# Up units of nine pairs per gated layer by Strassen's algorithm, all on VectorE, the x combinations made within the second pair

## The reference

```python
def _conv_glu_ffn(x, w_in, conv_w, conv_b, w_down):
    gate, up = jnp.split(x @ w_in, 2, axis=-1)
    gate = lax.conv_general_dilated(
        gate, conv_w[:, None, :], window_strides=(1,),
        padding=[(CONV_WIDTH // 2, CONV_WIDTH // 2)],
        ..., feature_group_count=FFN_DIM) + conv_b
    return (jax.nn.gelu(gate, approximate=False) * up) @ w_down

for i in range(DEPTH):
    ...
    h = _conv_glu_ffn(x, f_w_in[i], f_conv_w[i], f_conv_b[i], f_w_down[i])
    x = _layer_norm(DEEPNORM_ALPHA * x + h, ln_g[i, 1], ln_b[i, 1])
```

## Time and profile before

| | |
|---|---|
| median of 3 runs | 1276.72 us (1276.08 to 1278.55) |
| the profiled execution | 1277.31 us, its span 1275.6 us |
| TensorE busy | 1266.0 us (99%), 6096 matmuls |
| VectorE busy | 650.2 us (51%) |
| ScalarE busy | 459.4 us (36%) |
| GpSimd busy | 165.1 us (13%) |
| DMA, mean | 110 GB/s |

### The profile page before, as it was taken

The page is one execution under the profiler, slowest core; times in us unless marked ns, Lnnn a source line. Parts: engine busy times, 40 slices in busy tenths (PEclk is TensorE's granted clock), DMA queues, the critical chain, the costliest instruction groups (busy, mean ns, idle before and its releaser), DMA issues.

```text
span 1275.6 us, 15660 instructions
## 1 busy us (share of the span) xinstructions
PE 1266.0 (99%) x6096; PEld 1055.6 (83%) x6096; DVE 650.2 (51%) x890; ACT 459.4 (36%) x553; POOL 165.1 (13%) x159
## 2 busy tenths in 40 slices
PE   9999999999999999999999999999999999999997
PEld 7888888889888888888888877788988888888886
DVE  3637877346343434433372777775743334343346
ACT  3422333322232323322314588775143222232230
POOL 3001100040000000000224444453100000000001
PEclk9999999999999999999999999999999999999999
DMA  8434564250433232222522334235032333232221
GB/s 269 146 96 124 173 176 147 89 185 2 131 99 99 87 99 80 98 97 99 188 74 71 100 105 124 91 108 166 33 99 99 99 99 99 99 99 100 96 102 66
DMA packets 104652, 140.64 MB, mean 110 GB/s; under 512 B 9440, under 2 KB 81464, under 8 KB 104352
## 3 DMA queue, kind: packets, MB, share of 16 engines
q1 hardware_dynamic: 95024, 127.81, 31.2%
q0 software_dynamic: 9440, 12.11, 2.9%
q10 hardware_dynamic: 144, 0.13, 0.0%
HBM read 137.85 MB, written 10.52 MB: 116 GB/s over the span
## 4 chain that ended last, share of the span: by engine, by line
PE 98%; DVE 1%; DMA 0%; ACT 0%; issue 0%; POOL 0%; DVEq 0%; SPq 0%; POOLq 0%
PE bank L1263 31%; PE bank L1267 31%; PE bank L1266 31%; PE bank L1654 1%; PE bank L1508 1%; PE bank L1273 1%; PE bank L1406 1%; DMA w_raw<-in_a_w_in_dram 0%; PE bank L1511 0%; PE bank L1397 0%; DVE prob L1141 0%; DVE w_lo L875 0%; PE bank L1684 0%; PE bank L1683 0%; ACT w_hi L514 0%
## 5 line engine op out<-in xcount | busy, mean ns | idle before, releaser
L1263 PE MATMUL bank<-xt_hi,w_hi 128*128 128x512 f32 (+1 forms) x1008 | 380.8, 378 | 0.0
L1267 PE MATMUL bank<-xt_hi,w_lo 128*128 128x512 f32 (+1 forms) x1008 | 378.8, 376 | 0.0
L1266 PE MATMUL bank<-xt_lo,w_hi 128*128 128x512 f32 (+1 forms) x1008 | 378.7, 376 | 0.0
L765 DVE TENSOR_TENSOR w_lo<-w_raw,w_hi 128x2048 fp32r<-128x2048 f32 x79 | 180.8, 2289 | 184.6 <-ACT w_hi L468 158.3
L1263 PEld LDWEIGHTS bank<-xt_hi,w_hi 128*128 128x128 f32 x1008 | 189.7, 188 | 36.4 <-issue 3.0
L1267 PEld LDWEIGHTS bank<-xt_hi,w_lo 128*128 128x128 f32 x1008 | 189.7, 188 | 34.5
L1266 PEld LDWEIGHTS bank<-xt_lo,w_hi 128*128 128x128 f32 x1008 | 189.8, 188 | 33.9
L468 ACT CAST w_hi<-w_raw 128x2048 fp32r<-128x2048 f32 x53 | 101.3, 1913 | 185.6 <-PE bank L1263 179.6
L1263 PE MATMUL bank<-w_hi,s_hi 128*128 128x512 f32 x416 | 162.1, 390 | 0.0
L1266 PE MATMUL bank<-w_lo,s_hi 128*128 128x512 f32 x416 | 161.9, 389 | 0.0
L1267 PE MATMUL bank<-w_hi,s_lo 128*128 128x512 f32 x416 | 161.8, 389 | 0.0
(11 more groups left out here) (209 smaller groups left out, 1488.3 us busy)
## 6 DMA issues: line engine op xcount, KB each, us to landing
w_raw<-in_f_w_in_dram SPq DMA_DIRECT2D x44, 1024.0 KB, 5.1
w_raw<-in_f_w_down_dram SPq DMA_DIRECT2D x22, 1024.0 KB, 4.8
w_raw<-in_a_w_in_dram SPq DMA_DIRECT2D x14, 1024.0 KB, 6.1
bias_by_query_key<-bias_by_distance POOLq DMA_DIRECT2D x8, 1024.0 KB, 16.0
w_raw<-in_a_w_out_dram SPq DMA_DIRECT2D x8, 1024.0 KB, 7.0
w_raw<-in_b_w_qkv_dram SPq DMA_DIRECT2D x16, 512.0 KB, 4.8
bias_sb<-bias_by_query_key SPq DMA_DIRECT2D x32, 256.0 KB, 2.6
w_raw<-in_b_w_qkv_dram SPq DMA_DIRECT2D x4, 1024.0 KB, 5.4
```

Of the source, the lines that this page charges most:

```text
L765: dve.tensor_tensor(lo_of(u), w_raw[:, u % 2, :], hi_of(u), ALU.subtract).then_inc(w_lo_done, 1)
L1263: ins = pe.matmul(o, a_hi, b_hi, start=start, stop=False)
L1266: pe.matmul(o, a_hi, b_lo, start=False, stop=False)
L1267: return pe.matmul(o, a_lo, b_hi, start=False, stop=stop)
```

## The change

The first two pairs of each gated layer stay as they are (`PLAIN = 2`). In the other nine the up unit is one product of 2 x 2 cells: the weights [256 columns x 1024 rows] as cells A of 128 columns by 512 rows, x as cells of 512 rows by 256 tokens, the result as four quarters of 128 columns by 256 tokens. By Strassen's algorithm (Winograd's form) it takes seven cell products instead of eight, each 4 row chunks x 3 matmuls of 256 columns (`multiply`, banks 2 to 7 and again 2).

- Per pair VectorE makes four sums of weight cells (`sums`) and seven low parts (`lows`); ScalarE makes seven high parts and copies the first product (M1). VectorE adds the other products up out of PSUM into `act` (`add`, seven additions, the last one in the next pair), and multiplies `act` by the GELU in place (`gated`) in the next pair, between the sums and the low parts.
- Once per layer VectorE makes four combinations of x cells, T1 to T4, 1024 elements per partition each, in 10 operations that each wait for the one before; ScalarE makes their high parts and VectorE their low parts. In VectorE's queue the combinations stand in the second pair, behind the low part of its up unit and before its taps, the low parts behind the right taps and before the low part of the third gate unit. In ScalarE's queue the four high parts stand before the middle taps of the second pair.
- The loops are over seven pairs instead of ten, with the first and last of the nine written out. The down projection's start also waits for the sixth addition of the last pair.

Loads, the gate units and all other stages are unchanged. The diff, cut to its core:

```diff
+    w_sum = at("w_sum", 80 * KB, [P, 2, UC])
+    more_hi = [at(f"more_hi{k}", R_U + (72 + 2 * k) * KB, [P, NB], F32R) for k in range(3)]
+    more_lo = [at(f"more_lo{k}", R_U + (78 + 2 * k) * KB, [P, NB], F32R) for k in range(3)]
+    more_sum = [at(f"more_sum{k}", R_U + (78 + 2 * k) * KB, [P, NB]) for k in range(3)]
+    COMB = [R_U + 48 * KB, R_U + 56 * KB, 112 * KB, R_U + 64 * KB]
+    comb_hi = [at(f"comb_hi{k}", COMB[k], [P, KD // 2, 2 * P], F32R) for k in range(4)]
+    comb_lo = [at(f"comb_lo{k}", COMB[k] + 4 * KB, [P, KD // 2, 2 * P], F32R) for k in range(4)]
+    comb_part = [at(f"comb_part{k}", COMB[k], [P, KD // 2, 2 * P]) for k in range(4)]
+    comb = [at(f"comb{k}", COMB[k] + 4 * KB, [P, KD // 2, 2 * P]) for k in range(4)]
...
+        A11, A12, S1, S2, S4, S3, A22 = range(7)
+        T1, T2, T3, T4 = range(4)
+        M1, M2, M6, M7, M5, M3, M4 = range(7)
+        PLAIN = 2
+        NV = FB // 2 - PLAIN
+        def cell_sum(par, m):
+            return w_sum[:, par, NB * m:NB * m + NB] if m < 4 else more_sum[m - 4][:, :]
...
+        def raw_cell(par, b, a):
+            return w_raw[:, par, :].rearrange("p (k n) -> p k n", n=2 * P)[:, 4 * a:4 * a + 4, P * b:P * b + P]
+        def x_cell(xt, a, s):
+            return xt[:, 4 * a:4 * a + 4, 2 * P * s:2 * P * s + 2 * P]
+        def cell_bank(m):
+            return bank[(2, 3, 4, 5, 6, 7, 2)[m]][:, 0:2 * P]
...
+                def group(g):
+                    if g:
+                        weights_at(u0 + 2 * g + 1)
+                        for k in (T1, T2, T3, T4):
+                            act_e.wait_ge(comb_done, 4 * l + k + 1)
+                            act_e.copy(comb_hi[k][:, :, :], comb[k][:, :, :]).then_inc(comb_hi_done, 1)
...
+                    weights_at(u0 + 2 * g + 2)
+                    for j in range(2):
+                        gelu(2 * g + j, j)
...
+                    act_e.wait_ge(w_landed[par], landed_count(u) + (0 if i is None else i * 16))
+                    act_e.wait_ge(w_used, u - 1 + (0 if i is None else i * 2))
+                    for m, k in ((A11, 0), (A12, 1)):
+                        act_e.copy(as_cell(cell_hi(par, m)), raw_cell(par, 0, k)).then_inc(cell_hi_done, 1)
+                    for n, m in enumerate((S1, S2, S4, S3)):
+                        act_e.wait_ge(sum_done, count(l, 4, v, n + 1, i))
+                        act_e.copy(cell_hi(par, m), cell_sum(par, m)).then_inc(cell_hi_done, 1)
+                    act_e.copy(as_cell(cell_hi(par, A22)), raw_cell(par, 1, 1)).then_inc(w_hi_done, 1)
+                    for j in range(2):
+                        middle(f + j, j)
+                    act_e.wait_ge(cells_mm, count(l, 7, v, 1, i))
+                    act_e.copy(quarter(v, i, 1, 1), cell_bank(M1)).then_inc(m1_copied, 1)
+                    weights_at(u + 1, i)
+                    if v == NV - 1:
                         stationary(act, None, 0, act_done, f0 + 2)
+                    for j in range(2):
+                        gelu(f + j, j)
...
+                def step(ins, n):
+                    ins.then_inc(comb_step, 1)
+                    dve.wait_ge(comb_step, 6 * l + n)
+                def combine(k, hi, lo, n):
+                    whole, part = comb[k][:, :, :], comb_part[k][:, :, :]
+                    if k in (T1, T3):
+                        step(dve.tensor_tensor(whole, x_cell(xt_hi, *hi), x_cell(xt_hi, *lo), ALU.subtract), n)
+                        step(dve.tensor_tensor(part, x_cell(xt_lo, *hi), x_cell(xt_lo, *lo), ALU.subtract), n + 1)
+                        dve.tensor_tensor(whole, whole, part, ALU.add).then_inc(comb_done, 1)
+                    else:
+                        step(dve.tensor_tensor(whole, x_cell(xt_hi, *hi), comb[lo][:, :, :], ALU.subtract), n)
+                        dve.tensor_tensor(whole, whole, x_cell(xt_lo, *hi), ALU.add).then_inc(comb_done, 1)
+                    dve.wait_ge(comb_done, 4 * l + k + 1)
+                def group(g):
+                    if g:
+                        weights(u0 + 2 * g + 1)
+                    if g == 1:
+                        dve.wait_ge(up_mm, 2 * PLAIN * l + 2)
+                        combine(T1, (0, 1), (0, 0), 1)
+                        combine(T2, (1, 1), T1, 3)
+                    if g == 1:
+                        combine(T3, (1, 1), (0, 1), 4)
+                        combine(T4, (1, 0), T2, 6)
                     for j in range(2):
+                        left(2 * g + j, j)
                     for j in range(2):
+                        right(2 * g + j, j)
+                    if g == 1:
+                        for k in (T1, T2, T3, T4):
+                            dve.wait_ge(comb_hi_done, 4 * l + k + 1)
+                            dve.tensor_tensor(comb_lo[k][:, :, :], comb[k][:, :, :], comb_hi[k][:, :, :], ALU.subtract
+                                              ).then_inc(comb_lo_done, 1)
+                    weights(u0 + 2 * g + 2)
+                    for j in range(2):
+                        dve.wait_ge(gelu_done, f0 + 2 * g + 1 + j)
+                        dve.wait_ge(up_mm, 2 * PLAIN * l + 2 * g + 1 + j)
+                        dve.tensor_tensor(act[:, 2 * g + j, :], conv[:, j, :], bank[2 + j][:, :], ALU.mult
+                                          ).then_inc(act_done, 1)
+                def sums(v, i=None):
+                    u = u0 + 2 * (PLAIN + v) + 1
+                    par = u % 2
+                    dve.wait_ge(w_landed[par], landed_count(u) + (0 if i is None else i * 16))
+                    dve.wait_ge(w_used, u - 1 + (0 if i is None else i * 2))
+                    to = {m: as_cell(cell_sum(par, m)) for m in (S1, S2, S3, S4)}
+                    dve.tensor_tensor(to[S1], raw_cell(par, 1, 0), raw_cell(par, 1, 1), ALU.add).then_inc(sum_done, 1)
+                    dve.wait_ge(sum_done, count(l, 4, v, 1, i))
+                    dve.tensor_tensor(to[S2], to[S1], raw_cell(par, 0, 0), ALU.subtract).then_inc(sum_done, 1)
+                    dve.wait_ge(sum_done, count(l, 4, v, 2, i))
+                    dve.tensor_tensor(to[S4], raw_cell(par, 0, 1), to[S2], ALU.subtract).then_inc(sum_done, 1)
+                    dve.tensor_tensor(to[S3], raw_cell(par, 0, 0), raw_cell(par, 1, 0), ALU.subtract).then_inc(sum_done, 1)
+                    dve.wait_ge(sum_done, count(l, 4, v, 4, i))
+                def lows(v, i=None):
+                    u = u0 + 2 * (PLAIN + v) + 1
+                    par = u % 2
+                    for n, m in enumerate((A11, A12, S1, S2, S4, S3)):
+                        dve.wait_ge(cell_hi_done, count(l, 6, v, n + 1, i))
+                        hi, lo = cell_hi(par, m), cell_lo(par, m)
+                        if m in (A11, A12):
+                            ins = dve.tensor_tensor(as_cell(lo), raw_cell(par, 0, m - A11), as_cell(hi), ALU.subtract)
+                        else:
+                            ins = dve.tensor_tensor(lo, cell_sum(par, m), hi, ALU.subtract)
+                        ins.then_inc(cell_lo_done, 1)
+                    dve.wait_ge(w_hi_done, u + 1 + (0 if i is None else i * 2))
+                    dve.tensor_tensor(as_cell(cell_lo(par, A22)), raw_cell(par, 1, 1), as_cell(cell_hi(par, A22)),
+                                      ALU.subtract).then_inc(w_lo_done, 1)
+                def add(v, i, to, have, m, after=0):
+                    if after:
+                        dve.wait_ge(cells_read, count(l, 7, v, after, i))
+                    dve.wait_ge(cells_mm, count(l, 7, v, m + 1, i))
+                    dve.tensor_tensor(to, have, cell_bank(m), ALU.add).then_inc(cells_read, 1)
+                def last_add(v, i=None):
+                    add(v, i, quarter(v, i, 1, 0), quarter(v, i, 1, 0), M4)
...
+                    if v:
+                        last_add(v - 1, i)
+                    sums(v, i)
+                    if v:
+                        gated(v - 1, i)
+                    lows(v, i)
+                    left(f, 0)
+                    left(f + 1, 1)
+                    right(f, 0)
+                    dve.wait_ge(m1_copied, count(l, 1, v, 1, i))
+                    add(v, i, q11, q22, M2)
+                    right(f + 1, 1)
+                    add(v, i, q12, q22, M6)
+                    weights(u + 1, 0 if i is None else i * 2)
+                    add(v, i, q21, q12, M7, 2)
+                    add(v, i, q12, q12, M5)
+                    add(v, i, q22, q21, M5, 3)
+                    if v == NV - 1:
                         stationary(act, S_D[l], 0)
+                    add(v, i, q12, q12, M3, 4)
...
+                def multiply(v, i, m, w, x_hi, x_lo, frees=0):
+                    u = u0 + 2 * (PLAIN + v) + 1
+                    hi, lo = as_cell(cell_hi(u % 2, w)), as_cell(cell_lo(u % 2, w))
+                    if w == A22:
+                        unit_ready(u, 0 if i is None else i * 2)
+                    else:
```

(83 more changed lines are left out.)

75 lines of the change are left out of this document (46 added, 29 removed).

## The result

The changed kernel takes 1280.3 us in the median (before 1276.8 beside it); the ratio is 1.0027 with a 95% interval of 1.0015 to 1.0040. It is slower by about a quarter of a percent, 3.4 us; 1280.4 had been forecast. Run again (`after_again`): 1279.99 us, ratio 1.0022 (1.0012 to 1.0032). The profile shown is that of `after_again`, since in the execution profiled first the array ran at half its rate from end to end (2535.7 us); that execution and one of the kernel before (1580.1 us) are left out of these medians.

The account below looks back on a forecast made before the run. TensorE's matmul slots were taken to bound the kernel. Strassen gain -14.7, stalls +13.8 and clock +4.6 gave +3.7 us: 1280.4 us against the median, range 1276.5 to 1286 (1273 to 1286 with rival 1).

Parts of the forecast that it names:

- What bounds the kernel, and the gain: TensorE's matmul slots bound the kernel; Strassen up units save 0.82 us a pair, 18 pairs, -14.7 us.
- A pair fits beside TensorE: In each Strassen pair VectorE's added work hides beside TensorE, 0 us; smallest slack 2.7 us, period 20.94 us.
- The stall: Before each layer's third gate unit TensorE waits 6.9 us for a low part queued behind the x combinations: +13.8 us.
- The clock: After each stall TensorE's clock is low for a while, costing 2.3 us a layer: +4.6 us, bounds 0 to 4.6 a layer.
- The sum: Whole kernel: -14.7 + 13.8 + 4.6 = +3.7 us, 1280.4 us against the median; forecast's chance 60%.
- rival 1: Same stalls before the third gate units but no fall of the clock: 1275.8 us, no change; 20%.
- The range: Whole kernel: 1276.5 to 1286 us, with clock loss 0.5 to 4.6 and stall 6.3 to 8.3 us a layer.
- Rival 2: In the second pair VectorE's combinations are fast enough that no stall forms: 1262 us; 10%.
- Rivals 3 and 4: Cost in every pair: VectorE bounds it, 1289 us, 7%; or products' waits are met late, 1288 us, 3%.

Follow-up runs that it names:

- halves: The kernel before with up units of the second to eleventh pair per gated layer as 96 matmuls of 256 columns instead of 48 of 512; 1289.72 us.
- spread: The changed kernel with the same operations reordered: the third gate unit's low part right behind the taps, most x combination work after it; 1262.74 us, ratio 0.9888.
- low_part_3x: Kernel spread with the low part of each gate unit that a Strassen pair makes computed three times; 1321.21 us, ratio 1.0355.
- lows_behind: The changed kernel with the third gate unit's low part moved ahead of all four low parts of the x combinations; 1267.60 us, ratio 0.9924.
- two_ahead: The changed kernel with the third gate unit's low part moved ahead of only the last two combination low parts; 1276.24 us, ratio 0.9992.
- before_combos: The kernel before plus only the x combinations with their high and low parts, read by nobody, in the change's queue places; 1295.62 us, ratio 1.0147.
- low_part_2x: Kernel spread with the low part of each gate unit that a Strassen pair makes computed twice; 1270.03 us, ratio 0.9947.

## Why the prediction was right

- *What bounds the kernel, and the gain.* Right. 18 pairs at 0.82 us were forecast; the period of 20.98 in place of 20.94 makes it 0.78, -14.0 us. `halves` shows that the term came from the right rows (20 units cost 12.6 us more, 12.4 expected from them): with 256 columns at half the price of 512 the nine pairs of each layer would have been worth 24 us.
- *A pair fits beside TensorE.* Right in the result, no wait in the loop; the low part of the next gate unit ran from T + 15.9 as worked out (426.61, with the gate unit's start at about 410.7). Calling 2.7 us the smallest slack was wrong: by its own times the exit of the layer has 0.2 us, and `spread`'s trace shows 0.5.
- *The stall.* Right by place, cause and size. 6.9 us were forecast, 6.8 measured; ten combinations took 12.55 us (12.6), the taps began 19.0 us after the second gate unit (19.05).
- *The clock.* It fell, which the rows of before had left open. The term of 2.3 us a layer was too large: 2.0 in the first layer, 1.7 in the second. It was the middle of two bounds, 0 and 4.6, and no row supported the middle, so that it came near is luck in part. The falls in the other profiles cost from 1.7 to 3.0 us, none as much as 4.6. That this is because the start of the kernel was thin work was not tried.
The Trainium skill (TensorE: Matmul & The Clock Gate, Part 1: The HAM clock gate) warns of this return to the slow clock by an idle engine; the trace agrees, with 0.50 granted from 343 on.
- *The sum.* -14.0 + 13.6 + 3.7 = +3.3 us with the measured terms, against +2.8 (`after_again`, by the ratio) and +3.4 (first comparison); +3.7 was forecast. The gain was put 0.7 us too high and the losses 1.1 us too high, and these errors nearly cancel. The clock was the least sure term, and it decided between the forecast and rival 1 (1275.8).
- *The range.* The bounds named for stall and clock add up to 1275.6 to 1287.8, not to 1276.5 to 1286. The measured time lies inside either.
- *The rivals.* Rival 2, VectorE fast enough to hide the combinations: excluded, 1.22 us each. Rivals 3 and 4, a cost in each pair: excluded by the period. What they describe can be made, though: 4.6 us more on VectorE did it (`low_part_3x`).

What stays open: `spread` was run with four executions, and its ratio has an interval of 0.3 points; whether a few tenths of a microsecond more are lost at the layers' exits was not tried. Nor was it tried what decides whether a gap of 2 us brings the clock down.

## What to carry to other kernels

When an algorithm saves work on the busiest engine, list what each helper engine's queue holds in front of the next operand that this engine needs, above all at the one-time preparation: 17 us of work that was harmless in another order of the queue cost all of a gain of 14 us, because one 2.3 us operation stood behind it. Move the operation with the due date forward before touching the arithmetic. Price a shorter matmul by its spacing in a stream, not by its share of columns, and add the fall of the clock (1.7 to 3.0 us in these profiles) to the price of a stall of several microseconds. Look for the least room at the entry and the exit of a loop too, not only inside it.

## What the runs showed of the hardware

- Matmuls of fp32r operands with a weight load each are 0.2267 us apart with 512 columns and 0.1198 with 256, in the gated MLP and in the attention layer, with x or the weights moving: 512 and 256 columns take 0.2133 and 0.1067 us at 2.4 GHz, so both cost the same 13 ns more.
- The clock can fall after TensorE has resumed: in the profiled execution of `lows_behind` the gap was over at 342.06 and the window from 342 to 344 holds the fall; in the second layer the gap was over at 952.14 and the window from 953 to 955 holds it. A gap of 2.1 us costs its 2.1 us or nearly 4, by execution.
- At the very start the granted clock doesn't show the rate: in the kernel before, the windows from 8 to 10 us have 1.00, and the three matmuls of 512 columns at 8.90 are more than 0.43 us apart.
- The price of a fall varies with no change in the code around it: 2.0 and 1.7 us in the two layers of the changed kernel, 3.0 and 1.7 in `two_ahead`, 2.4 and 1.8 in `before_combos`, 1.7 and 1.7 in `lows_behind`.
- A wait of VectorE for its own forerunner costs 0.03 us in straight code (321.87 + 1.22 = 323.09 to 323.12). In the loop 0.17 us idle stands in front of the products with the GELU in each pair. That the awaited count is computed there does not by itself explain it: in `low_part_2x` the wait between the two low parts has a computed count too and costs 0.03 us (418.02 + 2.29 = 420.31 to 420.34). What makes the difference was not tried.
